# Query weights requested ahead of the residual's stores, top 16 taken half by half, both index lookups fused

## The reference, cut to what matters

```python
def peer_ffn(h, lp):
    q = (h @ lp['peer_wq']).reshape(b, t, PEER_HEADS, PEER_DQ)     # 8 heads, 256 wide
    keys = lp['peer_keys']                                         # (2, 8, 128, 128)
    s1 = jnp.einsum('bthd,hkd->bthk', q[..., :half], keys[0])
    s2 = jnp.einsum('bthd,hkd->bthk', q[..., half:], keys[1])
    v1, i1 = lax.top_k(s1, PEER_TOPK)                              # 16 of 128
    v2, i2 = lax.top_k(s2, PEER_TOPK)
    cand = (v1[..., :, None] + v2[..., None, :])                   # 256 sums
    cidx = (i1[..., :, None] * PEER_NKEYS + i2[..., None, :])
    top_s, pos = lax.top_k(cand, PEER_TOPK)                        # 16 of 256
    eidx = jnp.take_along_axis(cidx, pos, axis=-1)
    gates = jax.nn.softmax(top_s, axis=-1)
    # then: sum over experts of gate * gelu(u_e . x) * v_e
```

## Time and profile before

| | |
|---|---|
| median of 3 runs | 3846.21 us (3845.15 to 3848.89) |
| profiled execution, own time | 3848.05 us |
| its span, first to last instruction | 3846.3 us |
| granted TensorE clock, mean | 0.962 |
| PE / PEld busy | 3542.8 us (92%) / 3129.1 us (81%) |
| DVE busy | 2902.8 us (75%) |
| ACT / POOL busy | 1177.5 us (31%) / 1160.3 us (30%) |
| routing, first query matmul to last key score | 1465.5 to 1719.6 us |

### The profile page before, as it was taken

One profiled execution on the slowest core, in us unless ns is written; L12 is line 12 of the kernel. 1 busy time (PEld: TensorE's weight loads), 2 busy tenths in 40 slices (PEclk: granted clock), 3 DMA queues, 4 the chain that ended last, 5 costly groups with the idle time before them and its releaser, 6 DMA issues.

```text
span 3846.3 us, 59039 instructions
## 1 busy us (share of the span) xinstructions
PE 3542.8 (92%) x20968; PEld 3129.1 (81%) x20968; DVE 2902.8 (75%) x3762; ACT 1177.5 (31%) x1890; POOL 1160.3 (30%) x986
## 2 busy tenths in 40 slices
PE   7999999999995996985699999999999999999887
PEld 3688888888884773444699999999999999999885
DVE  2565665665665222999699999999999999999987
ACT  1222321322232212115733333333333333333331
POOL 1444444444440734002022222222222222223230
PEclk9999999999997998997999999999999999999998
DMA  9433333333333422212789999999999999999985
GB/s 387 149 118 124 115 122 114 113 123 123 117 118 125 186 90 99 76 65 90 220 337 373 369 364 379 373 368 373 377 364 373 373 368 375 372 367 375 350 350 226
DMA packets 229754, 950.05 MB, mean 247 GB/s; under 512 B 22274, under 2 KB 63682, under 8 KB 154306
## 3 DMA queue, kind: packets, MB, share of 16 engines
q1 hardware_dynamic: 172098, 542.47, 38.8%
q0 software_dynamic: 55296, 402.68, 26.9%
q10 hardware_dynamic: 2304, 4.20, 0.3%
HBM read 914.55 MB, written 33.60 MB: 247 GB/s over the span
## 4 chain that ended last, share of the span: by engine, by line
DVEq 18%; DVE 18%; issue 7%; ACT 4%; PE 3%; DMA 1%; ACTq 0%; POOLq 0%; SPq 0%
DVEq L1982 17%; DVE Ub L1980 7%; ACT UH L1204 3%; DVE acc_r L1988 3%; DVE UL L1208 2%; DVE VL L1944 2%; DVE acc_x L1988 1%; DVE GB L1950 1%; DMA Vb<-peer_v,stage 1%; ACT AHa L1891 1%; DVEq L1967 1%; PE PS L1829 1%; PE PS L1830 0%; PE PS L1831 0%; DMA VR<-peer_vt 0%
## 5 line engine op out<-in xcount | busy, mean ns | idle before, releaser
L1222 PE MATMUL PS<-xh,UH 128*128 128x320 f32 x2048 | 633.3, 309 | 17.6 <-POOL UL L1208 17.6
L1830 PE MATMUL PS<-AL,VH 128*128 128x320 f32 x2048 | 644.1, 314 | 0.0
L1223 PE MATMUL PS<-xl,UH 128*128 128x320 f32 x2048 | 633.6, 309 | 0.0
L1224 PE MATMUL PS<-xh,UL 128*128 128x320 f32 x2048 | 633.4, 309 | 0.0
L370 PE MATMUL PS<-hH,WH 128*128 128x512 f32 (+1 forms) x1312 | 484.9, 370 | 8.4 <-ACT kk L685 7.4
L1782 POOL DMA_INDIRECT Vb<-peer_v,stage x192 | 243.0, 1266 | 770.8 <-DVE acc_r L1988 515.2
L371 PE MATMUL PS<-hL,WH 128*128 128x512 f32 (+1 forms) x1312 | 464.9, 354 | 0.0
L372 PE MATMUL PS<-hH,WL 128*128 128x512 f32 (+1 forms) x1312 | 463.8, 354 | 0.0
L1829 PE MATMUL PS<-AHa,VH 128*128 128x320 f32 x1024 | 327.9, 320 | 97.9 <-DVE AL L1954 70.2
L1222 PEld LDWEIGHTS PS<-xh,UH 128*128 128x128 f32 x2048 | 385.2, 188 | 17.8 <-issue 17.8
L1782 POOL DMA_INDIRECT Ub<-peer_u,stage x192 | 223.1, 1162 | 581.3 <-DVE Ub L1980 533.7
(11 more groups left out here) (331 smaller groups left out, 7269.4 us busy)
## 6 DMA issues: line engine op xcount, KB each, us to landing
UR<-peer_ut SPq DMA_DIRECT2D x128, 1024.0 KB, 6.6
VR<-peer_vt SPq DMA_DIRECT2D x256, 512.0 KB, 6.7
AW<-wada SPq DMA_DIRECT2D x128, 512.0 KB, 3.5
WR<-wseq SPq DMA_DIRECT2D x224, 256.0 KB, 2.6
wr<-wmod SPq DMA_DIRECT2D x32, 1024.0 KB, 10.5
gates_dram<-GS SPq DMA_DIRECT2D x10, 2048.0 KB, 8.9
GB<-gates_dram SPq DMA_DIRECT2D x32, 640.0 KB, 6.7
oR<-wout SPq DMA_DIRECT2D x32, 512.0 KB, 3.3
```

What stands on the lines that cost most here:

```text
L1222: pe.matmul(dst, UH[:, j % 2, k, :], xh[:, k, :], start=(k == 0), stop=False)
L1223: pe.matmul(dst, UH[:, j % 2, k, :], xl[:, k, :], start=False, stop=False)
L1224: last = pe.matmul(dst, UL[:, j % 2, k, :], xh[:, k, :], start=False, stop=(k == KT - 1))
L1830: pe.matmul(low, VH[:, slot, j, cols], AL[:, :, b, :], start=False, stop=False)
```

## The change

Three edits in `b3`. First, SyncE asks for the query weights of head 1 between the stores of `x1`: half 0 ahead of the first store, half 1 ahead of the third. The waits for `s_qpe` are the same as before. Second, VectorE's first `top16` is called once per half, with four groups each, behind a wait for that half's scores only. The arrays of values and indices have the half as their outer dimension now. One operation adds the candidates of all four tiles. Third, the two lookups are one: each of its three operations covers both halves, 2048 elements per partition in place of 1024, and `oh` lies over `cand` and `cand2`.

```diff
-            oh = carve(4096, [P, LT, TOPK, TOPK])
+            oh = carve(3072, [P, 2 * LT, TOPK, TOPK])
...
-            vv = carve(6656, [P, LT, 2, TOPK])
-            ii = carve(6784, [P, LT, 2, TOPK], u32)
-            iif = carve(6912, [P, LT, 2, TOPK])
+            vv = carve(6656, [P, 2, LT, TOPK])
+            ii = carve(6784, [P, 2, LT, TOPK], u32)
+            iif = carve(6912, [P, 2, LT, TOPK])
...
-                    for t in range(LT):
-                        sp.wait_ge(s_x1, t + 1)
-                        sp.dma_start(x1_dram[t * P:(t + 1) * P, :], x1[:, t, :]).then_inc(s_spill, 16)
-                    with sp.Fori(1, PH) as n:
-                        for j in range(2):
-                            sp.wait_ge(s_qpe, 2 * n + j - 1)
-                            sp.dma_start(wqb[:, j, :, :], wq[2 * n + j]).then_inc(s_wq[j], 16)
+                    def next_queries(n, j):
+                        sp.wait_ge(s_qpe, 2 * n + j - 1)
+                        sp.dma_start(wqb[:, j, :, :], wq[2 * n + j]).then_inc(s_wq[j], 16)
+
+                    for j in range(2):
+                        next_queries(1, j)
+                        for t in range(2 * j, 2 * j + 2):
+                            sp.wait_ge(s_x1, t + 1)
+                            sp.dma_start(x1_dram[t * P:(t + 1) * P, :], x1[:, t, :]).then_inc(s_spill, 16)
+                    with sp.Fori(2, PH) as n:
+                        next_queries(n, 0)
+                        next_queries(n, 1)
...
-                        dve.wait_ge(s_sev, 2 * m + 4)
-                        dve.memset(gs, 0.0)
-                        top16([(sc[:, t, j, :], s2[:, t, j, :], vv[:, t, j, :], ii[:, t, j, :]) for t in range(LT) for j in range(2)])
-                        for t in range(LT):
-                            dve.tensor_tensor(cand[:, t, :].rearrange("p (a b) -> p a b", a=TOPK),
-                                              vv[:, t, 0, :].unsqueeze(2).to_broadcast([P, TOPK, TOPK]),
-                                              vv[:, t, 1, :].unsqueeze(1).to_broadcast([P, TOPK, TOPK]), ALU.add)
+                        for j in range(2):
+                            dve.wait_ge(s_sev, 2 * m + 3 + j)
+                            dve.memset(gs, 0.0)
+                            top16([(sc[:, t, j, :], s2[:, t, j, :], vv[:, j, t, :], ii[:, j, t, :]) for t in range(LT)])
+                        dve.tensor_tensor(cand.rearrange("p t (a b) -> p t a b", a=TOPK),
+                                          vv[:, 0, :, :].unsqueeze(3).to_broadcast([P, LT, TOPK, TOPK]),
+                                          vv[:, 1, :, :].unsqueeze(2).to_broadcast([P, LT, TOPK, TOPK]), ALU.add)
...
-                        for j in range(2):
-                            dve.tensor_tensor(oh.rearrange("p t k i -> p (t k) i"), flat(abf[:, j, :, :]).unsqueeze(2).to_broadcast([P, LT * TOPK, TOPK]),
-                                              iota16.unsqueeze(1).to_broadcast([P, LT * TOPK, TOPK]), ALU.is_equal)
-                            dve.drain()
-                            dve.tensor_tensor(oh, oh, iif[:, :, j, :].unsqueeze(2).to_broadcast([P, LT, TOPK, TOPK]), ALU.mult)
-                            dve.drain()
-                            dve.tensor_reduce(pairs[:, :, j, bass.ds(m * TOPK, TOPK)], oh, AX.X, ALU.add)
-                            dve.drain()
+                        dve.tensor_tensor(oh.rearrange("p n k i -> p (n k) i"),
+                                          abf.rearrange("p j t k -> p (j t k)").unsqueeze(2).to_broadcast([P, 2 * LT * TOPK, TOPK]),
+                                          iota16.unsqueeze(1).to_broadcast([P, 2 * LT * TOPK, TOPK]), ALU.is_equal)
+                        dve.drain()
+                        dve.tensor_tensor(oh, oh, iif.rearrange("p j t i -> p (j t) i").unsqueeze(2).to_broadcast([P, 2 * LT, TOPK, TOPK]), ALU.mult)
+                        dve.drain()
+                        dve.tensor_reduce(pairs[:, :, 0:2, bass.ds(m * TOPK, TOPK)].rearrange("p t j k -> p j t k"),
+                                          oh.rearrange("p (j t) k i -> p j t k i", j=2), AX.X, ALU.add)
+                        dve.drain()
```

## The result

The changed kernel takes 3814.05 us (median of 4 runs, 3810.95 to 3816.88), the kernel before 3847.55 in the runs beside it (3845.15 to 3850.86): ratio 0.9912, 95% interval 0.9895 to 0.9929, 33.5 us less. The forecast was 3812.8, and 33.4 less. The profiled execution of the changed kernel has a span of 3815.1 us (before 3846.3).

A forecast was written before the change was run, and what follows sets the result against it. TensorE's 17.42 us wait for query weights delays VectorE, which bounds the routing loop. Earlier candidates 24.5, per-head savings 1.7 and shorter stalls 7.25 sum to 33.4 us off 3846.21: 3812.8 us, range 3804 to 3825.

The forecast's parts named there:

- Query weights earlier: TensorE in head 0: no 17.42 us wait for head 1's query weights, so second scores start 19.8 us earlier.
- Halves as they come: VectorE in head 0 searches each half when its scores arrive; candidates come 24.5 us earlier, the largest term.
- The price of the split: VectorE, each head: four more drains cost 0.64 us, second wait, register step and memset 0.25; nearly all that fusing gives.
- Per head: VectorE's loop: 29.9 us per head instead of 30.04, giving 1.7 us from head 0's candidates to head 7's end.
- The stretched lookups: VectorE in heads 6 and 7: stalls behind GpSimd's low parts fall from 14.05 to 6.8 us, 7.25 us less.
- without any stall: Range's lower end: VectorE loses nothing to GpSimd in heads 6 and 7, gaining 40 us in all.
- free drains: VectorE's loop: if the further drains cost nothing, a head takes 29.3 us and the end comes some 5 us earlier.
- GpSimd first in head 6: Rival, 22%: GpSimd's low part starts before VectorE's multiply, which loses 4.55 us; gain 29.0 us, time 3817.
- The other way round in head 7: Rival, 11%: VectorE's multiply precedes waiting GpSimd, losing 1.25 us instead of 5.55; gain 37.7 us, time 3808.5.
- Searches blocked by GpSimd: Rival, 8%: VectorE's searches wait for GpSimd, candidates of head 0 come 10.9 us later; gain 18 us, time 3828.
- Given back later: Rival, 6%: something behind the routing is due at a fixed time and eats part or all of 33 us; 3846 at worst.
- The clock: Rival, 3%: TensorE without its pause drops to 1.2 GHz, 13.7 us more per query half; four slow halves give 3863.

The follow-up runs named there:

- e1: Kernel before with only the transfer order changed (query weights of head 1 requested between the residual's stores): 3827.37 us, ratio 0.9944.
- e10: Changed kernel with both scores ahead of the next queries, `xl` in eight pieces, low parts in four, both halves searched in one call: 3801.22 us, ratio 0.9879.
- e4: Changed kernel with both halves searched in one call of eight groups behind one wait: 3814.38 us, ratio 0.9911.
- e9: Changed kernel with both scores ahead of the next queries, `xl` in eight pieces and expert weights' low parts in four, halves searched separately: 3803.68 us, ratio 0.9891.
- e6: Changed kernel with TensorE making both halves' scores before the next head's queries: 3816.30 us, ratio 0.9922.
- e11: The changed kernel run again, unaltered, on the same chip as the last two variants: 3815.32 us, ratio 0.9915.
- e7: Changed kernel with both scores ahead of the next queries and GpSimd's `xl` in eight pieces instead of one operation: 3806.82 us, ratio 0.9902.
- e8: Changed kernel with each of GpSimd's low parts of the expert weights in four pieces: 3808.14 us, ratio 0.9904.
- e3: Changed kernel with the two lookups apart again, as two times three operations of 1024 elements: 3827.90 us, ratio 0.9947.

## Why the prediction was right

*Query weights earlier.* Forecast 19.8 us for the second scores; from the first query matmul to them it was 61.96 us and is 42.19. e1 has 19.7 at the end. Right in place and size, with the slow matmuls behind the wait as part of it.

*Halves as they come.* Candidates of head 0: 24.15 us earlier from the first query matmul on, 24.5 forecast. A half took 5.67 us in place of 5.35 at its second call in head 0; 0.29 of it is a gap in front of the first index search that other heads don't have. The price of the split was forecast as four drains of 0.16 and 0.25 for the second wait, 0.89; e10 and the changed kernel differ by 0.86 per head. The sentence that this price is nearly all that the fusing gives is borne out by e4. The forecast did not say the sharper thing that e4 shows: the halves as a whole are worth nothing here.

By the Trainium skill, "VectorE: DVE Perf Modes", § Rules for kernel authors, drains come anyway and only the number of operations counts. That is the drain which comes by itself behind each operation, not an instruction of the program. The number of searches is the same in e10 and e9, and those heads differ by 0.86 us: four drain instructions, one wait and one `memset` of four elements do cost that together. By the rows of the maxima (0.16 each) the drains are some 0.64 of it, an estimate, and no run here takes them out alone.

*Per head.* 29.9 forecast, 29.92 measured; with the last head 1.8 us in place of 1.7 over the loop.

*The stretched lookups.* 7.25 us forecast; 14.05 before, now 0.96 + 4.14 + 0.97 = 6.07, so 7.98. The order in head 6 was forecast by 0.18 us and came by 0.20. The gates' multiply was mis-sized: I let it lose 1.25 twice, it lost 0.96 and 0.97, and each time it ended 0.08 us behind GpSimd's operation.

24.15 + 1.8 + 7.98 = 33.95, against 33.4. That the forecast of the time is as close is partly luck: the runs of the changed kernel lie 6 us apart here, and those of the kernel before lie up to 14 us apart beside e1 to e4. Nearly all of that arises outside the routing, whose length was 286.05 and 285.98 in two executions of the changed kernel.

The lower end of the range was drawn short: 40 us without any stall give 3806, and the 5 us that the forecast itself put on free drains would make it 3801, not 3804.

*The rivals.* GpSimd first in head 6: not so, by 0.20 us; e6 shows what such a collision costs. The other way round in head 7: not so, GpSimd was waiting. Searches blocked by GpSimd: out, the first half's searches ran from 1498.9 to 1504.2 wholly beside GpSimd at 0.28 and 0.29 us each. Given back later: from the turned pairs to VectorE's last low part it is 1949.8 us before (to 3735.3) and 1952.5 in the profiled execution after, but 1950.0 in e11 and 1947.4 to 1953.0 over all runs; nothing is given back that can be told from this. The clock: 1.00 throughout.

By the Trainium skill, "SBUF — State Buffer", § SBUF: two separate sides, VectorE's two-input operations and GpSimd's lock each other out of a shared port pair for a whole instruction. e6, e7 and e8 agree: the wait lasts to the end of GpSimd's running instruction and is not a share of its load. The addition of e6 lost 5.0 us behind an instruction of 11.0, the cast of e7 lost 1.3 behind a piece of `xl` of 1.5, and the multiply of e8 lost 0.9 behind pieces of 1.3.

## What to carry to other kernels

Look for the first wait of the engine that feeds the bound, and at what stands in front of its transfer in the queue: here moving two requests past stores that nobody waited for gave 19.7 us. Where VectorE and GpSimd work at the same time, cut GpSimd's operations into pieces and join VectorE's two-input ones, and count the collisions and their lengths, not the busy time; then look at where the pieces end, since the pieces take longer in all and can meet what comes next. Splitting a search to start on the first half pays only if what it gains once, in the first turn, is more than its further drains and wait cost over all turns; if the producer can be reordered so that both halves come together, do that (e10, 6.4 us under e9).

## What the hardware showed that was not expected

A small cast or copy, an operation with one input, is blocked by GpSimd as well. In e10 VectorE ran, beside GpSimd's pieces in head 7 and behind the loop:

```profile
1716.28 1.30 DVE L1645 CAST ring<-ring 128x128 f32<-128x128 uint32 x1
...
1739.43 1.28 DVE L1677 COPY gate<-ring 128x128 f32<-128x128 f32 x1
```

The same cast takes 0.22 us in other heads, and the same copy 0.22 in the changed kernel. In e7 the cast behind the addition of head 0 lost 1.3 us the same way. So the line is not between one and two inputs, as the prediction had it: sums (2.29 us for 2048 elements), maxima, index searches and replaces go on beside GpSimd, a cast and a copy do not.

By the Trainium skill, "SBUF — State Buffer", § SBUF: two separate sides, a VectorE operation in a two-port mode takes the shared pair as well as one with two inputs. The blocked cast and copy fit that, and nothing here shows their mode.

TensorE's clock at the start of the queries differs between executions with the same work ahead of it. In e3, e9 and e10 the 64 matmuls of the first two query halves took 29.8 us, in the other ten executions 27.7. The window behind the first query matmul in e3, and that in e11:

```profile
1465.00:1494.00 29.00, 28.54 (x62) 12.68 (x63) 0.00 (x0) 8.93 (x6) 26.11 (x6) 0.92 0.46 158
```

```profile
1465.00:1494.00 29.00, 29.00 (x75) 13.34 (x74) 0.00 (x0) 9.71 (x7) 26.99 (x7) 1.00 0.49 158
```

Ahead of the queries TensorE turns the normalised rows in four spurts and idles 3.85 to 4.09 us between them, in each of these executions. The three differ from the others already there. From 24 to 12 us ahead of the first query matmul their mean granted clock is 0.78 and in the last 12 us it is 0.50, the lower level; in the other ten it is 0.50 and then 0.68. So in the three the clock had been up for a part of the earlier stretch, was down again when the queries began and stayed down for their first 4 us. All this lies ahead of the edited instructions. Why the clock takes one course or the other is open.
